# Products of 256 tokens in place of 512 in the input projection of a hybrid attention and recurrence block

## The chip, the cores and the metric

The kernel runs on one core of one Trainium2 chip. The metric is the device time of the whole kernel in microseconds (us). It stands at 877.26 us, the median of 3 runs (876.51, 877.26 and 878.25).

## What is computed

One block over 2048 tokens of width 1024: an RMS norm, an input projection to 3328 columns, a sliding-window attention with sinks beside an HGRN2 recurrence, an output projection, a second norm and the residual. The input projection is the matrix product that this case is about.

```python
h = rmsnorm(x, w_norm_pre[l])                 # x (1, 2048, 1024)
proj = h @ w_in[l]                            # w_in (1024, 3328)
q_a, k_a, v_a, z_a, q_r, f_r, i_r, z_r = jnp.split(proj, SPLIT_POINTS, axis=-1)
...                                           # attention and recurrence, each gated
y = jnp.concatenate([o_a, o_r], axis=-1) @ w_out[l]
x = x + rmsnorm(y, w_norm_post[l])
```

## The kernel before, in words

The tokens are worked through in four tiles of 512 (`N`, `TILES`, loop at L640). In each tile TensorE goes through 34 weight tiles of 1024 x 128 (`WT`): 26 of the input projection (`OUT0` = 26, loop at L661) and eight of the output projection (L677 to L711).

The arithmetic is float32, but done with rounded operands: each weight is held as a rounded part and a rest (`w_hi`, `w_lo`, type fp32r), and so are the normed activations (`h_hi`, `h_lo`). A product of a 128-row slice `k` is the sum of three matmuls, hi by hi, lo by hi and hi by lo. `products` (L473) issues one of them: the weights of slice k are the stationary operand (128 x 128), the activations of all 512 tokens the moving one, and the result adds up in one bank of PSUM over 24 products (`m` = 0 to 23: eight slices by three parts). The last product of a weight tile increments `tile_done`, for which ACT and DVE wait to read the bank. Each matmul of the program comes with a load of its stationary operand, which the profile shows as LDWEIGHTS on PEld.

`between` (L607) is called ahead of each product. At set places of the order, given by weight tile and m, it inserts the small matmuls of the other parts: attention scores and transposes (L507, L521, L531) and the recurrence's heads (L565, L575, L584, L587, L597). These use plain float32 operands but for L597 and L598; each plain float32 matmul of the code is two records of the profile, each with a load of its own. So four matmuls of the loop at L564 are eight records.

In tile 0 the first two weight tiles are multiplied in the order `ENTRY` (L643), slice by slice as the input arrives. From tile 1 on, weight tile 0 waits slice by slice for `h_lo`, and all others go through their 24 products with no wait but those ahead of the tile (L662 to L666) and those in `between`. ACT and DVE split the weights into parts in tile 0 and a little of tile 1; the parts are written to device memory and read back from there by SyncE's queue in the later tiles.

The order of everything is written out by hand, per engine; semaphores count the steps.

Of the kernel before, what the change touches and what calls it, by code (L numbers as in the profile page):

```python
# [32 lines left out]
N = 512  # L33
TILES = SEQ // N
KT = D_MODEL // P
# [43 lines left out]
def query(h):  # L79
    return H0 + 4 * h + 1  # L80
# [66 lines left out]
def hybrid_block(nc, x, x_rows, weights, cos, sin, vectors, w_post, squares, out, kept):  # L147
# [3 lines left out]
    with ctx:  # L151
# [72 lines left out]
        def acc(w):  # L224

            return bank[w % 4 if w <= query(0) else w % 3]
# [230 lines left out]
        def _(pe):  # L457
# [15 lines left out]
            def products(t, w, m, last):  # L473

                k, part = m // 3, m % 3
                s = SPLIT_SLOT[t * WT + w]
                stationary, moving = ((w_hi, h_hi), (w_lo, h_hi), (w_hi, h_lo))[part]
                mm = pe.matmul(acc(w)[:, :], stationary[:, s, k, :], moving[:, k, :],  # L478
                               start=(m == 0), stop=(m == 3 * KT - 1), skip_group_check=True)
                if last:  # L480
                    mm.then_inc(tile_done.sem, 1)

            def out_product(t, half, k, b, part):

                w = OUT0 + 4 * half + k // 2
                mix, weight = ((mix_hi, w_hi), (mix_lo, w_hi), (mix_hi, w_lo))[part]
                mm = pe.matmul(y_bank[half][b][:, :], mix[:, k, b * P:(b + 1) * P],  # L487
                               weight[:, SPLIT_SLOT[t * WT + w], (k % 2) * 4:(k % 2) * 4 + 4, :].rearrange("p a m -> p (a m)"),
                               start=(k == 0 and part == 0), stop=(k == KT - 1 and part == 2), skip_group_check=True)
                if k == KT - 1 and part == 2:  # L490
                    mm.then_inc(y_done.sem, 1)
                return mm
# [147 lines left out]
            for t in range(TILES):  # L640

                if t == 0:
                    for w, k, part in ENTRY:  # L643
                        if k == 0 and part == 0:
                            pe.wait_ge(y_read.sem, y_read.after(0, (2, 3)[w] - 8))
                            pe.wait_ge(hi_half[w], 1)
                        if k == 0 and part == 1:
                            pe.wait_ge(lo_half[w], 1)
                        if k == KT // 2 and part == 0:
                            pe.wait_ge(hi_split.sem, hi_split.after(0, w))  # L650
                        if k == KT // 2 and part == 1:
                            wait_split(pe, 0, w)
                        if w == K_TILE and part == 0:
                            for i in range(FILL.get(k, 0)):
                                pe.matmul(head_b[:, 0:P], ones, ones, start=True, stop=True)
                        if part == 0:
                            pe.wait_ge(h_hi_done.sem, h_hi_done.after(0, k))
                        if part == 2:
                            pe.wait_ge(h_lo_done.sem, h_lo_done.after(0, k))
                        products(t, w, 3 * k + part, 3 * k + part == 3 * KT - 1)  # L660
                for w in range(0 if t else V_TILE + 1, OUT0):  # L661
                    wait_split(pe, t, w)  # L662
                    if w < 4:
                        pe.wait_ge(y_read.sem, y_read.after(t, (2, 3, 1, 7)[w] - 8))
                    else:
                        pe.wait_ge(tile_read.sem, tile_read.after(t, w - (4 if w <= query(0) + 3 else 3)))  # L666
                    for m in range(3 * KT):
                        if w == 0 and m % 3 == 0:
                            pe.wait_ge(h_lo_done.sem, h_lo_done.after(t, m // 3))
                        between(t, w, m)  # L670
                        products(t, w, m, m == 3 * KT - 1)
# [7 lines left out]
                for i, (k, b) in enumerate(order):  # L679
                    for part in range(3):  # L680
# [8 lines left out]
                        mm = out_product(t, 0, k, b, part)  # L689
# [3 lines left out]
                for b in range(4):  # L693
                    for part in range(3):
                        mm = out_product(t, 0, KT - 1, b, part)

                if t + 1 < TILES:
                    for w in range(4):
                        wait_split(pe, t, OUT0 + 4 + w)
                        for b in range(4):  # L700
                            for k in (2 * w, 2 * w + 1):
                                for part in range(3):
                                    mm = out_product(t, 1, k, b, part)
# [721 lines left out]
```

## Time and profile before

| | before |
|---|---|
| median of the runs | 877.26 us |
| the profiled execution, first to last instruction (its span) | 872.4 us |
| TensorE matmul busy (PE) | 862.6 us, 99% |
| TensorE weight load busy (PEld) | 709.9 us, 81% |
| DVE busy | 592.9 us, 68% |
| ACT busy | 499.3 us, 57% |
| GpSimd busy (POOL) | 115.7 us, 13% |

The runs' times hold what lies around the span as well: the median is 4.9 us above the profiled span. Engines are named PE (matmul), PEld (the same engine's weight load, shown apart), DVE, ACT, POOL and SP. The end of a matmul is modelled and neighbouring matmuls overlap in the profile, so where TensorE is full, the distance from start to start tells what one costs, and its duration doesn't. L478 means line 478 of the kernel.

### The profile page before, as it was taken

How to read it: one execution, taken by the hardware profiler on the slowest of the kernel's cores; microseconds unless marked ns; L12 is line 12 of the kernel's file. 1: busy time of each engine (PE TensorE's matmuls, PEld its weight loads, DVE VectorE, ACT ScalarE, POOL GpSimd, SP SyncE). 2: the span in 40 equal slices, each digit the busy share in tenths (PEclk: the TensorE clock that was granted, in tenths of full speed). 3: DMA queues.
4: the chain of work that ended last, by engine and by line, in shares of the span. 5: the costliest groups of instructions: out<-in, count | busy, mean ns of one | idle time of the engine just before them, and what ended most of it. 6: DMA issues, size and time to landing. Idle time of an engine off the chain costs nothing.

```text
span 872.4 us, 12348 instructions
## 1 busy us (share of the span) xinstructions
PE 862.6 (99%) x4478; PEld 709.9 (81%) x4478; DVE 592.9 (68%) x1061; ACT 499.3 (57%) x1009; POOL 115.7 (13%) x90
## 2 busy tenths in 40 slices
PE   8999999999999999999999999999999999999997
PEld 6887788888888788888888878888888877788886
DVE  6878867764756798867163679878625468977823
ACT  7766456663574559657147546866624655667532
POOL 0000013430200001342020000243111000013112
PEclk9999999999999999999999999999999999999999
DMA  8685755639968544552785644446379545444463
GB/s 319 236 307 205 265 199 180 250 145 365 418 229 286 221 170 145 177 185 99 289 328 201 241 172 166 146 146 211 130 262 338 193 147 176 154 151 146 161 245 126
DMA packets 52924, 186.03 MB, mean 213 GB/s; under 512 B 5888, under 2 KB 6144, under 8 KB 52864
## 3 DMA queue, kind: packets, MB, share of 16 engines
q1 hardware_dynamic: 50128, 178.29, 57.2%
q10 hardware_dynamic: 2736, 6.95, 2.0%
q8 instruction: 36, 0.59, 0.3%
q14 instruction: 24, 0.20, 0.1%
HBM read 141.18 MB, written 44.04 MB: 212 GB/s over the span
## 4 chain that ended last, share of the span: by engine, by line
PE 88%; DVE 5%; DMA 3%; ACT 2%; issue 1%; SPq 1%; POOL 0%; DVEq 0%; ACTq 0%
PE bank L478 61%; PE bank L487 8%; PE score_b L487 4%; PE turn_b L487 4%; DMA kept_lo<-w_lo 2%; PE score_b L507 2%; PE turn_b L531 2%; PE turn_b L584 2%; PE bank L565 2%; PE turn_b L587 1%; PE bank L575 1%; DVE q_gate L1305 1%; PE turn_b L521 1%; DMA x_in<-in_x 1%; DVE w_lo L997 1%
## 5 line engine op out<-in xcount | busy, mean ns | idle before, releaser
L478 PE MATMUL bank<-h_hi,w_lo 128*128 128x512 f32 x832 | 327.1, 393 | 0.0
L478 PE MATMUL bank<-h_lo,w_hi 128*128 128x512 f32 x832 | 325.9, 392 | 0.0
L478 PE MATMUL bank<-h_hi,w_hi 128*128 128x512 f32 x832 | 324.5, 391 | 0.8 <-ACT h_hi L790 0.8
L478 PEld LDWEIGHTS bank<-h_lo,w_hi 128*128 128x128 f32 x832 | 156.3, 188 | 34.5 <-issue 3.3
L478 PEld LDWEIGHTS bank<-h_hi,w_hi 128*128 128x128 f32 x832 | 156.3, 188 | 33.6 <-ACT h_hi L790 1.3
L478 PEld LDWEIGHTS bank<-h_hi,w_lo 128*128 128x128 f32 x832 | 156.2, 188 | 33.1 <-issue 0.2
L1341 POOL TENSOR_TENSOR mix_lo<-v_r,mix_hi 128x512 fp32r<-128x512 f32 x16 | 21.2, 1323 | 522.6 <-ACT v_r L911 522.6
L997 DVE TENSOR_TENSOR w_lo<-w_raw,w_hi 128x1024 fp32r<-128x1024 f32 x37 | 45.8, 1248 | 32.8 <-ACT w_hi L736 32.6
L1119 DVE STREAM_TRANSPOSE kv_tok<-k_mid 32x128 f32<-32x128 f32 x192 | 58.0, 302 | 2.8
L736 ACT ACTIVATE w_hi<-w_raw 128x1024 fp32r<-128x1024 f32 x38 | 39.7, 1050 | 22.1 <-issue 9.9
L487 PE MATMUL bank<-w_hi,mix_lo 128*128 128x512 f32 x128 | 50.5, 395 | 0.0
L487 PE MATMUL bank<-w_hi,mix_hi 128*128 128x512 f32 x128 | 49.9, 389 | 0.0
L487 PE MATMUL bank<-w_lo,mix_hi 128*128 128x512 f32 x128 | 49.8, 389 | 0.0
L751 ACT ACTIVATE g_a<-g_a 128x512 f32<-128x512 f32 x32 | 20.2, 632 | 39.3 <-DVE g_a L1077 39.3
L740 ACT ACTIVATE g_a<-g_b 128x512 f32<-128x512 f32 x32 | 20.1, 629 | 38.7 <-DVE g_b L1073 38.7
L1325 POOL TENSOR_TENSOR x_acc<-x_acc,x_sq 128x512 f32<-128x512 f32 x21 | 32.5, 1545 | 71.6 <-ACT x_sq L786 71.6
L1077 DVE SCALAR_TENSOR_TENSOR g_a<-g_b,g_a 128x512 f32<-128x512 f32 x32 | 23.8, 742 | 23.7 <-ACT g_a L742 23.7
L850 ACT ACTIVATE f_b<-bank 32x512 f32<-32x512 f32 x48 | 28.3, 589 | 19.1 <-DVE q_gate L1305 10.6
L772 ACT ACTIVATE kv_tok<-f_d 32x128 f32<-32x128 f32 x96 | 29.5, 308 | 10.0 <-DVE f_d L1221 9.0
L1173 DVE TENSOR_TENSOR q_gate<-turn_b,w_post_t 128x512 f32<-128x512 f32 x8 | 5.5, 686 | 43.8 <-ACT f_c L797 43.8
L797 ACT ACTIVATE f_c<-turn_b 128x512 f32<-128x512 f32 x8 | 4.8, 594 | 46.3 <-PE turn_b L487 46.1
L772 ACT ACTIVATE probs<-f_d 32x128 f32<-32x128 f32 x96 | 29.5, 307 | 1.2
(189 smaller groups left out, 1467.4 us busy)
## 6 DMA issues: line engine op xcount, KB each, us to landing
w_hi<-kept_hi SPq DMA_DIRECT2D x96, 512.0 KB, 3.7
w_lo<-kept_lo SPq DMA_DIRECT2D x96, 512.0 KB, 4.7
w_raw<-in_weights SPq DMA_DIRECT2D x38, 512.0 KB, 5.4
kept_hi<-w_hi SPq DMA_DIRECT2D x34, 512.0 KB, 6.5
kept_lo<-w_lo SPq DMA_DIRECT2D x34, 512.0 KB, 7.1
x_in<-in_x_rows SPq DMA_DIRECT2D x8, 1024.0 KB, 7.2
x_in<-in_x SPq DMA_DIRECT2D x15, 512.0 KB, 5.9
out<-q_gate ACTq DMA_DIRECT2D x9, 512.0 KB, 8.5
```

The source lines that it names most:

```text
L478: mm = pe.matmul(acc(w)[:, :], stationary[:, s, k, :], moving[:, k, :], start=(m == 0), stop=(m == 3 * KT - 1), skip_group_check=True)
L487: mm = pe.matmul(y_bank[half][b][:, :], mix[:, k, b * P:(b + 1) * P], weight[:, SPLIT_SLOT[t * WT + w], (k % 2) * 4:(k % 2) * 4 + 4, :].re ...
L736: act.activation(w_hi[:, SPLIT_SLOT[i], :, :], w_raw[:, i % RAW_SLOTS, :, :], ACT.Copy).then_inc(hi_split.sem, 1)
L740: then(tile, act.activation(dst, src, ACT.Abs))
L751: act.activation(g_a[:, :], g_a[:, :], ACT.Exp).then_inc(gate_sig.sem, 1)
L772: copy = act.activation(square(v_tok(t, h), j, i), square(f_d[:, :], i, j), ACT.Copy)
L850: copy = act.activation(dst[32 * b:32 * b + 32, :], acc(s - 1)[32 * (b ^ 1):32 * (b ^ 1) + 32, :], ACT.Copy)
L997: dve.tensor_tensor(w_lo[:, s, :, :], w_raw[:, i % RAW_SLOTS, :, :], w_hi[:, s, :, :], ALU.subtract).then_inc(lo_split.sem, 1)
L1077: dve.scalar_tensor_tensor(g_a[:, :], g_b[:, :], 0.0, g_a[:, :], ALU.min, ALU.subtract).then_inc(gate_arg.sem, 1)
L1119: last = dve.transpose(square(kv_tok[:, 0, :], j, i), square(k_mid[:, :], i, j))
L1325: pool.tensor_tensor(x_acc[:, :], x_acc[:, :], x_sq[:, :], ALU.add).then_inc(x_added.sem, 1)
L1341: pool.tensor_tensor(o_sq_lo, o_sq[:, :], o_sq_hi, ALU.subtract).then_inc(o_low.sem, 1)
```

## The change

From tile 1 on, `products` issues each product as two matmuls, of tokens 0 to 255 and 256 to 511, with the same stationary operand, each with its own load of it. The two write the two halves of the same PSUM bank. The accumulation's start flag is on the first half of the first product alone; the increment of `tile_done` is on the second half of the last product. Tile 0 keeps one matmul of 512.

```diff
@@ -475,8 +475,14 @@
                 k, part = m // 3, m % 3
                 s = SPLIT_SLOT[t * WT + w]
                 stationary, moving = ((w_hi, h_hi), (w_lo, h_hi), (w_hi, h_lo))[part]
-                mm = pe.matmul(acc(w)[:, :], stationary[:, s, k, :], moving[:, k, :],
-                               start=(m == 0), stop=(m == 3 * KT - 1), skip_group_check=True)
+                if t == 0:
+                    mm = pe.matmul(acc(w)[:, :], stationary[:, s, k, :], moving[:, k, :],
+                                   start=(m == 0), stop=(m == 3 * KT - 1), skip_group_check=True)
+                else:
+
+                    for half in (slice(0, N // 2), slice(N // 2, N)):
+                        mm = pe.matmul(acc(w)[:, half], stationary[:, s, k, :], moving[:, k, half],
+                                       start=(m == 0 and half.start == 0), stop=(m == 3 * KT - 1), skip_group_check=True)
                 if last:
                     mm.then_inc(tile_done.sem, 1)
```

## Rows read from the trace of the kernel before

**Rows 1.** The page: busy us per engine; TensorE's granted clock in forty slices, tenths.

```profile
PE 862.6 (99%) x4478; PEld 709.9 (81%) x4478; DVE 592.9 (68%) x1061; ACT 499.3 (57%) x1009; POOL 115.7 (13%) x90
...
PEclk9999999999999999999999999999999999999999
```

**Rows 2.** The page: the chain that ended last, by engine and by line.

```profile
PE 88%; DVE 5%; DMA 3%; ACT 2%; issue 1%; SPq 1%; POOL 0%; DVEq 0%; ACTq 0%
PE bank L478 61%; PE bank L487 8%; PE score_b L487 4%; PE turn_b L487 4%; DMA kept_lo<-w_lo 2%; PE score_b L507 2%; PE turn_b L531 2%; PE turn_b L584 2%; PE bank L565 2%; PE turn_b L587 1%; PE bank L575 1%; DVE q_gate L1305 1%; PE turn_b L521 1%; DMA x_in<-in_x 1%; DVE w_lo L997 1%
```

**Rows 3.** Waits of TensorE: us in total, times, longest.

```profile
PE bank L639 <- DVE ones_r L999: 3.1, 1, 3.1
PE bank L478 <- ACT h_hi L790: 0.8, 2, 0.4
PE turn_b L531 <- ACT probs_t L763: 0.2, 1, 0.2
PE turn_b L466 <- DVE w_lo L997: 0.2, 1, 0.2
```

**Rows 4.** The chain in order of time, long pieces: start us, length us, what.

```profile
24.09 29.97 PE bank L478 x132
...
238.26 33.56 PE bank L478 x148
```

**Rows 5.** Timeline of PE in a quiet place of tile 2: start us, duration us.

```profile
453.68 0.39 PE L478 MATMUL bank<-h_hi,w_hi 128*128 128x512 f32 x1
...
454.36 0.39 PE L478 MATMUL bank<-h_hi,w_hi 128*128 128x512 f32 x1
...
454.81 0.39 PE L478 MATMUL bank<-h_lo,w_hi 128*128 128x512 f32 x1
```

**Rows 6.** Timeline of PEld, the weight loads, in the same place.

```profile
454.36 0.19 PEld L478 LDWEIGHTS bank<-h_hi,w_lo 128*128 128x128 f32 x1
```

**Rows 7.** Plain fp32 records, by line: duration ns min/median/max, first and last start.

```profile
L565 PE MATMUL bank<-q_even,k_mid x64: 275/275/377, 92.1 to 791.3; 128*128 128x128 f32 x64
L531 PE MATMUL turn_b<-probs_t,v_win x128: 379/379/430, 72.1 to 764.5; 128*64 128x256 f32 x128
L471 PE MATMUL turn_b<-x_acc,ones_r x2: 590/590/591, 23.1 to 23.5; 128*128 128x512 f32 x2
L540 PE MATMUL turn_b<-sq_in,v_t x4: 271/272/273, 53.9 to 54.2; 128*128 128x128 f32 x4
```

**Rows 8.** L478 in the same view; each of its three operand pairs has 832.

```profile
L478 PEld LDWEIGHTS bank<-h_hi,w_hi x832: 186/188/288, 5.9 to 818.9; 128*128 128x128 f32 x167
L478 PE MATMUL bank<-h_hi,w_hi x832: 387/389/766, 5.9 to 819.1; 128*128 128x512 f32 x167
```

**Rows 9.** The page: the instruction queue, packets, MB, share of 16 engines.

```profile
q8 instruction: 36, 0.59, 0.3%
```

**Rows 10.** Timeline of PEld in tile 1, loads of the head's small matmuls.

```profile
337.78 0.30 PEld L584 LDWEIGHTS turn_b<-a_t,kv_tok 128*128 128x128 f32 x2 [0.38 <-issue]
...
339.56 0.97 PEld L565 LDWEIGHTS bank<-v_t,k_mid 128*128 128x128 f32 x8
340.46 0.19 PEld L478 LDWEIGHTS bank<-h_lo,w_hi 128*128 128x128 f32 x1
```

**Rows 11.** Timeline of PE in tile 0, two more plain fp32 groups.

```profile
23.08 1.02 PE L471 MATMUL turn_b<-x_acc,ones_r 128*128 128x512 f32 x2
...
53.90 0.60 PE L540 MATMUL turn_b<-sq_in,v_t 128*128 128x128 f32 x4
```

**Rows 12.** Timeline of PE in tile 3, behind an insertion of small matmuls.

```profile
741.78 0.39 PE L478 MATMUL bank<-h_lo,w_hi 128*128 128x512 f32 x1
...
742.48 0.39 PE L478 MATMUL bank<-h_lo,w_hi 128*128 128x512 f32 x1
742.70 0.39 PE L478 MATMUL bank<-h_hi,w_hi 128*128 128x512 f32 x1
...
743.63 0.39 PE L478 MATMUL bank<-h_hi,w_lo 128*128 128x512 f32 x1
```

## The prediction

> **What bounds the kernel now.** I read the page first. TensorE is busy 99% of the span, and its granted clock is in the top tenth in every slice, the upper level (2.4 GHz) [rows 1]. A full TensorE row alone proves little, since the ends of matmuls are modelled, so the chain that ended last comes next: 88% of it is TensorE, 61% the one line that the change touches, L478 [rows 2]. The third view is the list of who waited for whom: TensorE waited 4.3 us in all, 3.1 of them once at the very start [rows 3]. DVE (68%) and ACT (57%) have room [rows 1]. So a nanosecond more on each product is a nanosecond on the end, and a nanosecond less is one won, as long as the others keep up.
>
> What sets the time of one product? Long unbroken stretches of the chain give the step from one product to the next: 29.97 / 132 = 0.2270 us and 33.56 / 148 = 0.2268 us [rows 4]. The timeline of a quiet place has the same step, 0.226 [rows 5], though each record is 0.39 us long: neighbours overlap by 0.16, so the step is the price and not the duration. The next load starts with the running matmul (454.36 in both views) and is 0.19 long [rows 5, 6]. Today it is wholly hidden.
>
> How much of 226.8 ns is columns? The plain fp32 records are 275 ns at 128 columns, 379 at 256 and 590 at 512 [rows 7]: (590 - 275) / 384 = 0.82 ns a column, two clocks at 2.4 GHz. The rounded operands of L478 have one clock, 0.417 ns: the record is 389 at 512 columns [rows 8], and 0.83 would not fit in its step. So 512 columns are 213.3 ns and 13.4 ns of each step are something else. The whole forecast is the question what becomes of these 13.4 ns.
>
> **The change, part by part.** Tiles 1 to 3 have 3 x 26 x 24 = 1872 products (the page's 3 x 832 = 2496 over four tiles [rows 8], three quarters of it). Removed: 1872 matmuls of 512 columns with a load each. Added: 3744 of 256 columns with a load each. Columns and result are the same, and the entry of tile 0, the output projection, the heads and every wait keep their place. The semaphore increment moves to the second half of the last product, which ends where the whole one ended. The DMA queues get no descriptor more, apart from the fetching of 3744 more instructions, which the instruction queue carries at 0.3% of the engines' time now [rows 9]; I cost that at nothing.
>
> Columns: 2 x 256 at 0.417 ns are again 213.3 ns. Cost: nothing.
>
> Loads: the cover of a load shrinks from a 227 ns step to one of some 110. Is that enough? The trace has chains in which each record needs 107 ns of columns (128 at 0.83) and its own 128x128 load: in the head's output and scores 16 loads start from 337.78 until just before 339.56, one in 1.78 / 16 = 0.111 us, and the eight of L565 behind them one in 0.90 / 8 = 0.112 [rows 10]. The load records are 0.19 us each there as well (0.30 for two) and overlap one another. So a load can be had every 111.5 ns, and a pair of half products costs at least 223 ns. This is the lower bound: 223 - 226.8 = -3.8 ns a product.
>
> The 13.4 ns: does it come once per matmul, or in proportion to the columns? Plain fp32 doesn't pay it. Two records of 512 columns at L471 stand (1.02 - 0.59) = 0.43 us apart for 427 of columns [rows 11], and four transposes of 128 columns (0.60 - 0.272) / 3 = 0.109 apart for 107 [rows 7, 11], so 2 to 3 ns for a record. Only the one-clock operands pay it. For once per matmul speaks that it isn't steady: after each insertion of small matmuls the step is larger for about eight products, (743.63 - 741.78) / 8 = 0.231 us, but one of the steps among them is 0.22 [rows 12]. A pure rate would not move; a bubble at each matmul's start or change of weights, which depends on how two streams of requests lie to each other, would. I take it as once per matmul. Then a half costs 106.7 + 13.4 = 120.1 ns, above the 111.5 of its load, so the load is still hidden, and a product costs 240.2: + 13.4 ns.
>
> The page "TensorE: Matmul & The Clock Gate" of the Trainium skill, section "Back-to-back issue gap", gives N / 2.4 + 2.5 ns at full clock. Its 215.8 ns for 512 columns is not what the rows here show (226.8). By it the change would add 2.5 ns a product, 4.7 us in all. The skill's "SBUF — State Buffer", section "Who interferes with whom", has two independent read ports for TensorE, one for moving data and one for weights; by that rule a doubled number of loads doesn't slow the columns. No row here tests this apart.
>
> **Sum.** 1872 x 13.4 ns = 25.1 us. The work between products keeps its forms; the first product behind it, with its load in the open, pays that load once, before and after. TensorE's waits on others in tiles 1 to 3 are under 1 us [rows 3], so there is nothing to absorb the growth, and the others only get more time. The span becomes 872.4 + 25.1 = 897.5 us. The median of the runs is 877.26, which is 4.9 above the profiled span, so the time is 902.4 us.
>
> **The rivals.**
> (a) The load's step decides and the surcharge is gone: 3.8 ns x 1872 = 7.1 us less, 870.2 us. For it: the chains of [rows 10] step at exactly this with as much column time and as many loads as the halves have. Against it: they are plain fp32, which doesn't pay the surcharge at 512 columns either (L471), so they don't tell that halves of rounded operands are rid of it.
> (b) The surcharge is in proportion: each half 113.4 ns, just above its load, 226.8 a product, no change, 877.3 us. For it: only operands read at full rate pay. Against it: the steps of [rows 12].
> (c) Between: a half pays the 2 to 5 ns that plain records pay over their columns [rows 10, 11] and its share of the rest, so 2 to 5 ns a product more, 4 to 9 us, 881 to 886 us. The Trainium skill's rule from "TensorE: Matmul & The Clock Gate" would come out at the lower end of this one.
> (d) Once per matmul, but never settled: with a load under way all the time, the steps stay as behind an insertion, 231 - 213.3 = 18 ns over the columns for each half. 2 x 18 - 13.4 = 22.6 ns a product, 42 us, 919.6 us. It decides if the regular step of [rows 5] needs the pause between one load's end and the next one's start (0.04 us), which the halves don't have.
> (e) Loads and columns don't overlap in halves: 111 + 107 = 218 a half, 436 a product, + 392 us. The chains of [rows 10], with both inside 111.5, speak against it. I give it 2 in 100, outside the range.
> That the change doesn't do what it says is hardly possible: a second half must be multiplied, and each matmul record has a load record beside it (832 and 832 [rows 8]).
>
> **How the numbers follow.** Once per matmul, 0.44 (898 to 907 us, its own range); (a) 0.17; (b) 0.15; (c) 0.10; (d) 0.12; (e) 0.02. The range must reach to (a) and to (d): 869 to 921 us leaves out the far part of each and (e). A measurement of this kernel tells 0.2%, 1.8 us, from no change. Faster: (a) and a little of (b) with its surcharge or its unsettled steps smaller, 0.20. Same: the rest of (b), 0.13. Slower: the remainder, 0.67.
>
> **What would show it.** In the profile after, TensorE still full at the upper clock level, L478 with 208 records of each operand pair at 512 columns and 1248 at 256, and the step of the 256-column records in a quiet place of tile 2: 0.120 confirms the surcharge per matmul, 0.1134 is (b), 0.1115 is (a), near 0.125 is (d). The length of tiles 1 to 3 should grow by 8.4 us each, all of it inside L478's stretches, while tile 0 and the output projection keep their length to 0.3 us; waits of TensorE on others stay under 2 us. The prediction is wrong if the halves' step falls outside 0.118 to 0.122, or if TensorE begins to wait for instructions or for another engine.

## The result and the profile after

The changed kernel takes 899.47 us (median of 3 runs, 898.62 to 900.12) against 877.26 before: a ratio of 1.0256, with a 95% interval of 1.0232 to 1.028. That is 22.2 us more, where 25.1 were forecast. The profiled execution spans 896.5 us, 24.1 more than before.

The page of the changed kernel, its parts 1, 2, 4 and 5, answers to [rows 1] and [rows 2]:

```profile
PE 886.9 (99%) x6350; PEld 812.2 (91%) x6350; DVE 594.4 (66%) x1061; ACT 499.4 (56%) x1009; POOL 114.9 (13%) x90
...
PEclk9999999999999999999999999999999999999999
...
PE 98%; DMA 1%; DVE 0%; ACT 0%; SPq 0%; DVEq 0%; issue 0%
...
L484 PE MATMUL bank<-h_hi,w_lo 128*128 128x256 f32 x1248 | 252.9, 284 | 0.0
...
L479 PE MATMUL bank<-h_hi,w_lo 128*128 128x512 f32 x208 | 82.8, 398 | 0.0
```

DVE and ACT do the same work in the same time; only TensorE's two rows have grown. Each operand pair has 1248 matmuls of 256 columns and 208 of 512, as the prediction asked. The chain that ended last is TensorE almost alone. The list of its waits has shrunk. It answers to [rows 3]; both entries lie in the first tile or ahead of it:

```profile
PE bank L645 <- DVE ones_r L1005: 3.1, 1, 3.1
PE bank L479 <- ACT h_hi L796: 1.0, 1, 1.0
```

L484 is the line with the halves; tile 0 keeps its products on L479. Next the timeline of the changed kernel in a quiet place of tile 2 (start us, duration us): PE, where each row is the two halves of one product, then PEld for the same place. They answer to [rows 5] and [rows 6].

```profile
464.75 0.40 PE L484 MATMUL bank<-h_hi,w_hi 128*128 128x256 f32 x2
464.99 0.40 PE L484 MATMUL bank<-h_hi,w_lo 128*128 128x256 f32 x2
...
465.71 0.40 PE L484 MATMUL bank<-h_hi,w_lo 128*128 128x256 f32 x2
...
464.87 0.31 PEld L484 LDWEIGHTS bank<-h_hi,w_lo 128*128 128x128 f32 x2
465.11 0.31 PEld L484 LDWEIGHTS bank<-h_lo,w_hi 128*128 128x128 f32 x2
```

From 464.75 to 465.71 there are four products, 0.240 us each: 0.120 a half. The loads now follow each other without a pause: each pair starts 0.24 us behind the one before and is 0.31 long. The pieces of the chain in order of time (start us, length us), which answer to [rows 4], give the same over a long stretch, 35.50 / 296 = 0.1199 us a half in tile 1 and 35.49 / 296 in tile 3:

```profile
240.07 35.50 PE bank L484 x296
...
682.59 35.49 PE bank L484 x296
```

The start of each tile, taken from the first product behind the output projection, was 226.3, 440.3 and 653.8 us before and is 227.9, 449.2 and 670.4 now. So tiles 1, 2 and 3 (the last one to the end of the span) grew from 214.0, 213.5 and 218.6 to 221.3, 221.3 and 226.1 us: + 7.3, + 7.8 and + 7.5, together 22.5 us, where the medians differ by 22.2. The other 1.6 us of the profiled span lie in tile 0, whose code is the same. They are scatter of its start: its first long piece of 132 products begins at 24.09 us before and at 25.70 now, and in the experiments below, all with the same tile 0, anywhere from 24.04 to 27.33 us.

### The profile page after: what moved, and what is told of

Same layout as the page of the kernel before. It is cut to its first block, busy times and chain, and to the rows that moved or that the text cites. A ratio compares the mean times of both kernels' runs of the same rounds, so it can differ in the third digit from the quotient of the medians.

```text
span 896.5 us, 16092 instructions
## 1 busy us (share of the span) xinstructions
PE 886.9 (99%) x6350; PEld 812.2 (91%) x6350; DVE 594.4 (66%) x1061; ACT 499.4 (56%) x1009; POOL 114.9 (13%) x90
## 4 chain that ended last, share of the span: by engine, by line
PE 98%; DMA 1%; DVE 0%; ACT 0%; SPq 0%; DVEq 0%; issue 0%
PE bank L484 50%; PE bank L479 16%; PE bank L493 10%; PE score_b L493 5%; PE turn_b L493 5%; PE score_b L513 2%; PE turn_b L537 2%; PE bank L571 2%; PE turn_b L590 2%; PE bank L581 2%; PE turn_b L593 1%; PE turn_b L527 1%; DMA x_in<-in_x 1%; PE score_b L604 0%; PE score_b L603 0%; PE score_b L557 0%
## 5 line engine op out<-in xcount | busy, mean ns | idle before, releaser
L484 PE MATMUL bank<-h_hi,w_lo 128*128 128x256 f32 x1248 | 252.9, 284 | 0.0
L484 PE MATMUL bank<-h_lo,w_hi 128*128 128x256 f32 x1248 | 252.7, 284 | 0.0
L484 PE MATMUL bank<-h_hi,w_hi 128*128 128x256 f32 x1248 | 251.5, 283 | 0.0
L484 PEld LDWEIGHTS bank<-h_lo,w_hi 128*128 128x128 f32 x1248 | 194.3, 192 | 2.3 <-issue 2.3
L484 PEld LDWEIGHTS bank<-h_hi,w_hi 128*128 128x128 f32 x1248 | 194.9, 192 | 0.5
L484 PEld LDWEIGHTS bank<-h_hi,w_lo 128*128 128x128 f32 x1248 | 194.3, 192 | 0.8
L479 PE MATMUL bank<-h_hi,w_lo 128*128 128x512 f32 x208 | 82.8, 398 | 0.0
L479 PE MATMUL bank<-h_hi,w_hi 128*128 128x512 f32 x208 | 81.7, 397 | 1.0 <-ACT h_hi L796 1.0
L479 PE MATMUL bank<-h_lo,w_hi 128*128 128x512 f32 x208 | 81.9, 394 | 0.0
L479 PEld LDWEIGHTS bank<-h_hi,w_hi 128*128 128x128 f32 x208 | 39.5, 190 | 9.4 <-ACT h_hi L796 1.3
L479 PEld LDWEIGHTS bank<-h_lo,w_hi 128*128 128x128 f32 x208 | 39.4, 189 | 9.0 <-issue 1.0
L479 PEld LDWEIGHTS bank<-h_hi,w_lo 128*128 128x128 f32 x208 | 39.4, 189 | 8.5 <-issue 0.2
L1331 POOL TENSOR_TENSOR x_acc<-x_acc,x_sq 128x512 f32<-128x512 f32 x21 | 31.6, 1503 | 73.6 <-ACT x_sq L792 73.6
```

What stands on the lines that cost most here:

```text
L484: mm = pe.matmul(acc(w)[:, half], stationary[:, s, k, :], moving[:, k, half], start=(m == 0 and half.start == 0), stop=(m == 3 * KT - 1), ...
L1331: pool.tensor_tensor(x_acc[:, :], x_acc[:, :], x_sq[:, :], ALU.add).then_inc(x_added.sem, 1)
```

## The experiments

The forecast rested on one statement: the rounded operands pay 13.4 ns a matmul over their columns, however many columns it has. Call it theory A, and the 13.4 ns the surcharge. (It is 13.3 or 13.4 as the step is taken as 226.7 or 226.8.) Three groups of runs test it: whether the growth is where it should be and of the size forecast for other splits, whether it has to do with the load, and whether it has to do with the operands.

**Only one tile.** Halves in tile 1 alone.

```diff
+for a, b in ((0, N // 2), (N // 2, N)) if t == 1 else ((0, N),):
+    mm = pe.matmul(acc(w)[:, a:b], stationary[:, s, k, :], moving[:, k, a:b],
...
```

> Only tile 1 has halves, tiles 0, 2 and 3 whole products. Theory A (each matmul record of the rounded operands costs 13.3 ns over its columns, wherever it stands): 624 products x 13.3 = 8.3 us, less some 0.8 us because the steps behind insertions are nearer to the settled one for halves: 884.7 us, a third of the change's 22 us. Rival B (the growth comes from the whole chain, such as fetching of instructions or the start): not a third of it.

Measured: 883.18 us against 876.69 for the kernel before, ratio 1.0078 (1.0061 to 1.0095): + 6.5 us, by its interval 5.3 to 8.3, where a third of the change is 7.4. The forecast for it, 884.7, was 1.5 us too high. In its profile tile 1 is 221.5 us long and tile 2 is 213.5 as before. Long pieces of its chain, tile 1 and then tile 2:

```profile
239.52 35.51 PE bank L479 x296
...
460.15 33.55 PE bank L479 x148
```

The same 148 products take 1.96 us more as halves, 13.2 ns each. About a third of the change's growth for a third of its products, and all of it in tile 1: A stands, and rival B, by which the growth comes from the whole chain, is out.

**No neighbours with the same weights.** For each slice the three parts of the first half, then the three of the second.

```diff
+elif part == 2:
+    for a, b in ((0, N // 2), (N // 2, N)):
+        for p, (stationary, moving) in enumerate(((w_hi, h_hi), (w_lo, h_hi), (w_hi, h_lo))):
+            mm = pe.matmul(acc(w)[:, a:b], stationary[:, s, k, :], moving[:, k, a:b],
...
```

> Halves from tile 1 on, but for each slice the three parts of the first half and then the three of the second, so that no two neighbouring matmuls have the same weights. Theory A (13.3 ns per matmul record): as the changed kernel, steps of 120.0 ns, 899 us. Rival C (a second load of the same weights is cheaper, or only a change of weights costs): steps over 120 ns; at 13.3 ns for each changed pair more, another 25 us, 924 us.

Measured: 897.82 us, ratio 1.0241 (1.0224 to 1.0258), within the changed kernel's own interval. Timeline of this kernel in tile 2:

```profile
464.93 0.28 PE L484 MATMUL bank<-h_hi,w_hi 128*128 128x256 f32 x1
465.05 0.28 PE L484 MATMUL bank<-h_hi,w_lo 128*128 128x256 f32 x1
...
465.53 0.28 PE L484 MATMUL bank<-h_lo,w_hi 128*128 128x256 f32 x1
```

Five steps in 0.60 us, 0.120 each. Whether two neighbours have the same weights makes no difference, so rival C is out.

**Uneven and finer splits.** The first has 384 and 128 tokens, the second four times 128.

```diff
+for a, b in ((0, 384), (384, N)) if t else ((0, N),):
```

> From tile 1 on each product is 384 and 128 tokens. Theory A with a load step of 111.5 ns as in the plain fp32 chains: 160.0 + 13.3 = 173.3 ns for the wide one, and for the narrow one (53.3 + 13.3 = 66.7) the load step of 111.5: 285 ns a product, 58 over the whole product, 877 + 1872 x 0.0581 - 2 = 984 us. Rival D (the halves' 120.0 ns is already the step of a rounded operand's load, and the columns' surcharge is something else): 173.3 + 120.0 = 293.3 ns, 1000 us.

> From tile 1 on each product is four matmuls of 128 tokens. Theory A with a load step of 111.5 ns: 446 ns a product, 1872 x 0.2193 = 411 us more, 1286 us. Rival D (load step of 120.0): 480 ns a product, 474 us more, 1350 us. If loads were no bound at all: 4 x 66.7 = 267 ns a product, 952 us.

Measured: 984.30 us for 384 and 128 (ratio 1.1228, 1.1211 to 1.1245), and 1286.07 us (one run) for four times 128. Long pieces of the chain, first of 384 and 128:

```profile
491.63 42.37 PE bank L479 x296
```

then of four times 128:

```profile
601.25 66.06 PE bank L479 x592
```

42.37 / 148 = 286.3 ns a product and 66.06 / 148 = 446.4 ns. Theory A with the load's step from [rows 10] had 285 and 446, and 984 and 1286 us. Rival D, by which the halves' 120 ns were already the step of the load, had 1000 and 1350 and is out: a load of rounded weights can be had every 111.6 ns, like one of plain fp32. The halves lie above that by 8 ns, the quarters lie on it.

**Fewer weight columns in the load.** If the surcharge were the load's reading in the way of the columns' reading, a shorter load would lower it. That is rival E of the first two expectations, and theory F of the later ones. The runs load and multiply only the first 64, 96 or 32 weight columns in slices 1 to 7, from tile 1 on; the cut shown is of the first of them.

```diff
+rows = slice(0, P if t == 0 or k == 0 else P // 2)
+mm = pe.matmul(acc(w)[rows, a:b], stationary[:, s, k, rows], moving[:, k, a:b],
...
```

> Whole products of 512 tokens, but from tile 1 on and for slices 1 to 7 only 64 of the 128 weight columns are loaded and multiplied, so the upper 64 outputs of each weight tile lack these slices. The load reads half as much. Theory A (13.3 ns per matmul record, whatever is loaded beside it): settled step 226.7 ns as before. Rival E (the surcharge is the load's reading getting in the way of the columns' reading, 13.3 ns for 128 weight columns): 6.7 ns for 64, settled step 220.0 ns.

> As the run before, with halves: slices 1 to 7 load 64 weight columns and leave the upper 64 outputs without these slices. Theory A: step 120.0 ns. Rival E: 113.3 ns. Rival D (the halves' 120.0 is the step of the load): a load of 64 is far shorter, the step falls to 106.7 plus what the columns cost, at or under 120.

> Slices 1 to 7 with fewer weight columns, so some outputs lack them: tile 1 has 96 of 128 with 512 tokens, tile 2 has 32 with 512, tile 3 has 64 with 384 tokens (the last 128 tokens lack the slices). Theory A: 226.7, 226.7 and 173.3 ns. Theory F (an eighth slower while a load is read): 213.3 + 10.0 = 223.3, 213.3 + 3.3 = 216.7 and 160.0 + 6.7 = 166.7 ns. The run with 64 columns and 512 tokens spoke against both with 229.8; if that is a rule (the steps never settle when the load is short and leaves a long pause), the 96 are settled near 226.7 or at 230, and the 32 at 230.

> Slices 1 to 7 in halves of 256 tokens with 96 weight columns in tile 1 and 32 in tile 2; in tile 3 one matmul of 192 tokens with all 128 weight columns (outputs and tokens left out lack the slices). Theory F: 106.7 + 10.0 = 116.7 and 106.7 + 3.3 = 110.0 ns. Theory A: 120.0 and 120.0. The 192 tokens: 80.0 + 13.3 = 93.3 ns is below the load's 111.5, so 111.5 by both.

The first of these took 878.36 us and the second 877.01, beside 874.77 for the kernel before, one run each; the other two have a different form in each tile (865.42 and 872.06 us in all, beside 876.75), so their steps are what counts. Timeline with 64 weight columns and 512 tokens:

```profile
470.98 0.40 PE L480 MATMUL bank<-h_lo,w_hi 128*64 128x512 f32 x1
...
471.68 0.39 PE L480 MATMUL bank<-h_lo,w_hi 128*64 128x512 f32 x1
471.91 0.39 PE L480 MATMUL bank<-h_hi,w_hi 128*64 128x512 f32 x1
472.13 0.39 PE L480 MATMUL bank<-h_hi,w_lo 128*64 128x512 f32 x1
...
472.82 0.40 PE L480 MATMUL bank<-h_hi,w_lo 128*64 128x512 f32 x1
```

Eight steps in 1.84 us are 0.230 each, single ones from 0.22 to 0.24. This is the restlessness of [rows 12], and here it lasts through the whole stretch. Now 64 weight columns in halves:

```profile
475.97 0.39 PE L480 MATMUL bank<-h_hi,w_lo 128*64 128x256 f32 x2
...
476.88 0.39 PE L480 MATMUL bank<-h_lo,w_hi 128*64 128x256 f32 x2
```

Four products in 0.91 us, 0.114 a half. And with 32 weight columns and 512 tokens, in tile 2 of the third run:

```profile
489.92 0.40 PE L480 MATMUL bank<-h_hi,w_hi 128*32 128x512 f32 x1
...
491.31 0.40 PE L480 MATMUL bank<-h_hi,w_hi 128*32 128x512 f32 x1
```

Six steps in 1.39 us, 0.232 each. I took the mean step over all such records of each form, the long first steps behind insertions left out (at 128 weight columns it is the settled value), and what it is above the columns at 0.4167 ns:

| weight columns loaded | 512 tokens: step, surcharge (ns) | 384 tokens | 256 tokens |
|---|---|---|---|
| 128 | 226.7, 13.3 | 173.3, 13.3 | 120.0, 13.3 |
| 96 | 230.1, 16.7 | | 116.2, 9.5 |
| 64 | 229.8, 16.5 | 173.3, 13.3 | 113.7, 7.0 |
| 32 | 231.8, 18.5 | | 117.8, 11.1 |

Neither theory is right as it stands. Theory F says that the surcharge falls with the load at any width. It meets 256 columns with 96 and 64 weight columns (116.7 and 113.3 forecast). It misses 32 there (110.0), 384 with 64 (166.7), and all of 512, where the steps rise with shorter loads. Theory A says that the surcharge stays. It meets 384 with 64, and misses the halves, where the surcharge falls to 7 ns at 64 weight columns. What holds is narrower: with a full load of 128 it is 13.3 ns at the widths of this table, and with shorter loads anything from 7 to 19 ns.

With 64 weight columns halving doesn't double it either. Two halves take 2 x 113.7 = 227.4 ns and the whole product 229.8, so there the split costs nothing; the two runs' times show no cost of it either. "Once per matmul" is shown for full loads and for no others.

**Other widths with a full load.** One matmul a product, slices 1 to 7 with the first 320, 384 or 448 tokens only.

```diff
+rows, cols, step = ((P, N, N), (P, 320, 320), (P, 384, 384), (P, 448, 448))[t] if k else (P, N, N)
+for a in range(0, cols, step):
+    mm = pe.matmul(acc(w)[0:rows, a:a + step], stationary[:, s, k, 0:rows], moving[:, k, a:a + step],
...
```

> One matmul a product, all 128 weight columns loaded, but slices 1 to 7 stream only the first 320 tokens in tile 1, 384 in tile 2 and 448 in tile 3; the other tokens lack these slices. Is the surcharge the same 13.3 ns at every width? Theory A (per record) and theory F (the columns run an eighth slower while a load of 128 is read, 107 ns of it in each record) both say 146.7, 173.3 and 200.0 ns. In proportion to the columns (17 for 16) it would be 141.7, 170.0 and 198.3 ns.

The whole took 856.92 us with the work left out. In this run TensorE waits for other engines (15.5 us on one line of ACT alone), and in parts of it the granted clock is at its lower level. The two places shown are at a granted clock of 1.00. Timelines of tile 1 and tile 2:

```profile
260.01 0.30 PE L480 MATMUL bank<-h_hi,w_hi 128*128 128x320 f32 x1
...
261.91 0.31 PE L480 MATMUL bank<-h_hi,w_lo 128*128 128x320 f32 x1
...
490.25 0.33 PE L480 MATMUL bank<-h_hi,w_lo 128*128 128x384 f32 x1
...
491.46 0.33 PE L480 MATMUL bank<-h_lo,w_hi 128*128 128x384 f32 x1
```

13 steps in 1.90 us are 146.2 ns (the mean of all 320-column records is 146.6), and 7 in 1.21 us are 172.9 ns. Per matmul has 146.7 and 173.3, in proportion has 141.7 and 170.0. At 448 columns the steps hardly settle: their mean is 202.9 ns, where per matmul has 200.0 and in proportion 198.3, so this width fits neither well. Proportion is out at 320 and 384. The 192-column records in tile 3 of the fourth run with short loads step at 110.7 ns at the upper clock level, near the load's step again.

The run with other widths shows its matmuls at the lower level too. TensorE had stood idle for 4 us, and from 242.4 to 246.2 us its granted clock is 0.50, which is 1.2 GHz:

```profile
241.29 0.79 PE L466 MATMUL turn_b<-mix_hi,ones_r 128*128 128x512 f32 x1 [4.02 <-DVE w_lo L999]
...
243.59 0.47 PE L480 MATMUL bank<-h_hi,w_hi 128*128 128x320 f32 x1
...
246.26 0.46 PE L480 MATMUL bank<-h_hi,w_lo 128*128 128x320 f32 x1
```

Ten steps in 2.67 us are 267 ns each, and 320 columns at 1.2 GHz are 266.7 ns: nothing is left over. So the 13.3 ns aren't a fixed number of TensorE's clocks at the start of each matmul, for these would be 26.7 ns here. In these runs the surcharge is seen at 2.4 GHz only.

**Other operands.** The products' operands are exchanged for constants (zeros and ones) in bf16, in whole products and in halves; a last run has bf16 with 64 weight columns in tile 1, with 128 in tile 2, and rounded fp32 from two fixed addresses in tile 3.

```diff
+mm = pe.matmul(acc(w)[:, a:b], half_words(ident[:, 0:P // 2]), half_words(reset[:, a // 2:b // 2]),
...
```

> From tile 1 on the products multiply constants read as bf16 (the identity as weights, a vector of zeros and ones as moving data) in place of weights and activations: 128x128 by 128x512, same count, same banks; the products' results are left out. It halves the bytes read per column. If the 13.3 ns belong to reading four bytes a clock (theory A's cause): the step falls to 213.3 plus 2 to 3 ns as plain fp32 has it, 216 ns. If they belong to the matmul's start or to writing PSUM every clock: 226.7 ns.

> The same constants in bf16, in halves of 256 columns. If the surcharge belongs to reading four bytes a clock: 106.7 plus 2 to 3 ns, or the load's step of 111.5 where that is longer, so 109 to 112 ns. If it belongs to the start of each matmul or to PSUM: 120.0 ns.

> Slices 1 to 7 with other operands of 512 columns, the products' results left out: tile 1 bf16 constants with 64 weight columns (a load that isn't of the short kind the 128-column bf16 loads had, 98 ns), tile 2 the same with 128, tile 3 rounded fp32 as in the kernel but the same two addresses every time (ones as weights, slice 0 as moving data). If four bytes a clock are what costs: tiles 1 and 2 at 215.8 ns, tile 3 at 226.7. If it is the load's reading time: tile 1 over 215.8 by half of 13.3 or so, 222 ns. If fixed addresses alone made the bf16 steps short: tile 3 at 215.8 as well.

Measured, one run each: 860.47, 862.97 and 875.66 us (before beside them: 874.77, 874.77, 876.75). Bf16 in halves, a long piece of the chain:

```profile
449.06 32.33 PE bank L486 x296
```

Bf16 in whole products of 512 columns, timeline and then the group by line (duration ns min/median/max):

```profile
459.78 1.67 PE L486 MATMUL bank<-reset,sq_in 128*128 128x512 bf16 x7
...
L486 PEld LDWEIGHTS bank<-reset,sq_in x1872: 95/98/101, 227.2 to 805.3; 128*128 128x128 bf16 x188
```

The last run, timelines of bf16 with 64 weight columns and of the fixed addresses:

```profile
259.73 2.54 PE L481 MATMUL bank<-reset,sq_in 128*64 128x512 bf16 x11
...
706.28 1.98 PE L484 MATMUL bank<-h_hi,ones_r 128*128 128x512 f32 x8
```

A group's length is its steps and the length of its last record. Whole bf16: (1.67 - 0.38) / 6 = 0.215 us. Halves: 32.33 / 296 = 0.1092. With 64 weight columns: (2.54 - 0.38) / 10 = 0.216, where a cost of the load's reading was forecast at 0.222. Fixed addresses: (1.98 - 0.39) / 7 = 0.227. So bf16 pays 2.5 ns over its columns, whole or in halves, and rounded fp32 pays 13.3 with fixed addresses too. A load of 98 ns instead of 188 isn't the reason by itself, since with rounded operands a shorter load brought the step of 512 columns up and not down. Nor are fixed addresses. So the surcharge goes with the rounded fp32 operands. One thing was changed along with the type and isn't told apart: the bf16 runs stream zeros and ones, and the run with fixed addresses streams the kernel's own activations.

## Why the prediction was right, point by point

**What bounds the kernel** held: the 22.5 us that tiles 1 to 3 grew by reached the end, and no other engine took a part of them. TensorE's waits in these tiles are gone from the list.

**The columns** cost the same in two halves, and **the load** stays hidden in halves: the bound of 111.5 ns from the small matmuls of [rows 10] is what the quarters then showed for rounded operands, 111.6. That row carried two further forecasts to within a microsecond (984 and 1286 us).

**The 13.4 ns** was the step on which all hung, and I took it as once per matmul. It is: 226.7 became 240.0, with 120.0 for each half against the 120.1 forecast. 1872 x 13.3 = 25.0 us. The changed kernel doesn't pay all of that, and this is the term of the sum that was mis-sized, by 2.5 us. I summed the steps between neighbouring product records of tiles 1 to 3, and what they are above the settled step:

- The first step behind an insertion, in 36 places, is long by 3.5 us in all before and by 3.2 after: the load in the open, about the same both times, as the prediction has it.
- The other steps are 1.2 us above the settled 226.7 before [rows 12] and 0.4 us below the settled 120.0 in halves, since a half behind an insertion mostly steps at 112 to 120 ns. With the first item that is 4.7 us before and 2.9 after, 1.8 us less.
- The distance from the last product of a stretch to the inserted matmul behind it is 73.6 ns over a settled step on average before and 55.0 after, in 39 places: 0.7 us less, of which some 0.4 are the waits of TensorE on DVE and ACT in [rows 3], which are gone.

25.0 - 1.8 - 0.7 = 22.5 us, the growth of the three tiles. The prediction had said that the places of insertion cost the same before and after, and that was the wrong part: it priced the change by its settled step alone. It also put the growth at 8.4 us a tile, where 7.3 to 7.8 were measured, and tile 0 at 0.3 us, where its start alone scatters by 3.

**The reason given for "once per matmul"** doesn't carry it. It was the restless steps of [rows 12], which a pure rate would not show. But with 64 weight columns and 512 tokens the steps are restless from end to end, and there two halves cost no more than the whole. So restless steps don't tell whether halving doubles the surcharge; with full loads it did, and in that the choice of "once per matmul", at 0.44, had some luck in it. The prediction's other guess, a bubble at each start or change of weights, isn't shown: the run with the parts apart excludes only a discount for equal weights, and the stretch at 1.2 GHz has no surcharge at all. And loads and columns aren't independent for these operands, since the step depends on the load's width, in different directions at 256 and at 512 columns.

**The rivals.** (a) had the load's step decide: out, since 120.0 lies 8 ns above it. (b), in proportion: out by the halves and by the widths 320 and 384. (c), which splits the surcharge into a part per matmul and a share: out by the same rows. The Trainium skill, "TensorE: Matmul & The Clock Gate", section "Back-to-back issue gap", gives N / 2.4 + 2.5 ns for a single matmul by itself at full clock: the streams of the bf16 runs agree with it (215.8 and 109.2 by the rule, 0.215 and 0.1092 us measured), and the rounded fp32 runs don't (226.7 and 120.0). So the rule fits bf16 and understated the cost here. (d), steps that never settle in halves: out, they settle within about eight records. Its price was also too high: the 231 ns of [rows 12] is one place, and over all insertions the first ten ordinary steps behind one lie only 3 ns above 226.7. Steps that never settle are what short loads bring at 512 columns, but those aren't in this kernel. (e) out.

**What stays open** is the mechanism. A limit on reading four-byte operands, and how the load's requests lie to the columns', would fit the bf16 runs, the dependence on the load's width and the missing surcharge at 1.2 GHz, but no run shows it. No run here shows why the surcharge is 13.3 ns with a full load at 256, 320, 384 and 512 columns, or why a shorter load raises it at 512 columns and lowers it at 256. Nor is "once per matmul" told apart from a rounding-up: at 2.4 GHz 13.3 ns are 32 clocks, every width tried with a full load is a multiple of 64 columns, and a step rounded up to the next multiple of 32 clocks would look the same.

## What to carry to other kernels

Where TensorE is full, price a matmul by the distance from start to start in a quiet stretch, split it into columns and the rest, and ask of the rest whether it comes once per matmul: here, with full loads, it did, and halving the columns doubled it. Small matmuls elsewhere in the same trace, with as many loads and as much column time as the new ones, give the load's step and with it the width below which splitting becomes far dearer (here 111.6 ns, between 192 and 256 columns of rounded fp32). And a change that alters the settled step alters the unsettled ones behind each interruption too, so count the interruptions before taking settled step times count.

## What was not expected of the hardware

With rounded fp32 operands of 512 columns, less weight to load makes the matmul slower: 226.7 ns with 128 weight columns, 230 with 96 or 64, 232 with 32; at 256 columns 64 weight columns are best (113.7 ns) and 32 worse again (117.8). With full loads the step settles within ten matmuls after an interruption; at 512 columns with short loads it does not in the stretches seen. Bf16 pays 2.5 ns where rounded fp32 pays 13.3, and at the lower clock level rounded fp32 pays nothing over its columns (267 ns for 320 of them).
